# DeltaNet inverse at levels 4 and 5: packed diagonal 64x64 blocks, and all four turns behind all four y products

## The reference

```python
CHUNK = 64
kb = k * beta[..., None]
lmat = jnp.where(strict, jnp.einsum('nbhid,nbhjd->nbhij', kb, k) * decay, 0.0)
amat = lmat + jnp.eye(CHUNK, dtype=F32)
rhs = jnp.concatenate([v * beta[..., None], kb * jnp.exp(gcum)[..., None]], axis=-1)
sol = lax.linalg.triangular_solve(amat, rhs, left_side=True, lower=True, unit_diagonal=True)
u, w = sol[..., :dv], sol[..., dv:]
def step(s, xs):
    v_new = u_i - jnp.einsum('bhcd,bhde->bhce', w_i, s)
    o = jnp.einsum('bhcd,bhde->bhce', qg_i, s) + jnp.einsum('bhij,bhje->bhie', attn_i, v_new)
    s = s * gl_i[..., None, None] + jnp.einsum('bhcd,bhce->bhde', kd_i, v_new)
    return s, o
```

## Time and profile before

| | us |
|---|---|
| median of 3 runs | 3374.56 (3374.05 to 3378.11) |
| profiled execution, own time | 3373.96 |
| its span, first to last instruction | 3372.1 |
| TensorE busy | 3216.7 (95%) |
| VectorE busy | 2492.9 (74%) |
| ScalarE busy | 1346.5 (40%) |
| GpSimd busy | 277.0 (8%) |
| first DeltaNet layer, first y product to last oi product | 565.6 to 679.1 |
| second DeltaNet layer, the same | 2905.1 to 3018.5 |

### The profile page before, as it was taken

How to read it: one execution, slowest core, us unless ns; L and a number is a source line. 1 busy time by engine, 2 the same in 40 slices (tenths; PEclk the granted TensorE clock), 3 DMA queues, 4 the chain that set the end, 5 groups by cost and what they waited for, 6 DMA issues and landing times.

```text
span 3372.1 us, 50038 instructions
## 1 busy us (share of the span) xinstructions
PE 3216.7 (95%) x17956; PEld 2998.1 (89%) x17956; DVE 2492.9 (74%) x4217; ACT 1346.5 (40%) x2398; POOL 277.0 (8%) x373
## 2 busy tenths in 40 slices
PE   7999898989999999899999999999999999899997
PEld 7899898979999998868999998899999898888997
DVE  7888976667887885567887887788788886666444
ACT  2333556243334334354334333433433365533332
POOL 1000004510000000000000000000000000640000
PEclk9999999999999999999999999999999999999999
DMA  7555310044544553214553554355445431013331
GB/s 292 218 198 211 142 71 1 26 163 187 205 181 187 218 205 136 102 41 185 204 219 142 207 218 160 147 198 216 181 187 208 160 129 52 26 48 134 120 122 75
DMA packets 66032, 515.99 MB, mean 153 GB/s; under 512 B 8144, under 2 KB 16336, under 8 KB 18048
## 3 DMA queue, kind: packets, MB, share of 16 engines
q1 hardware_dynamic: 60512, 493.12, 38.0%
q0 software_dynamic: 5408, 21.37, 1.7%
HBM read 509.65 MB, written 4.82 MB: 153 GB/s over the span
## 4 chain that ended last, share of the span: by engine, by line
PE 87%; DVE 7%; ACT 2%; issue 1%; DMA 1%; SPq 0%; POOL 0%; DVEq 0%; POOLq 0%; ACTq 0%
PE bank L1774 76%; PE bank L1964 5%; DVE xhat L1359 1%; DMA mod_raw<-mod_w 1%; DVE x L1363 1%; PE bank L1970 1%; PE bank L2072 1%; DVE split_lo L1209 1%; PE bank L1915 1%; DVE mod_junk L434 1%; PE bank L1822 0%; DVE xS_lo L1302 0%; PE bank L1826 0%; DVE blocks L1478 0%; PE bank L1823 0%
## 5 line engine op out<-in xcount | busy, mean ns | idle before, releaser
L1774 PE MATMUL bank<-xS_hi,split_hi 128*128 128x386 f32 (+2 forms) x3280 | 1120.2, 342 | 13.5 <-DVE gate_n L1325 10.2
L1774 PE MATMUL bank<-xS_hi,split_lo 128*128 128x386 f32 (+2 forms) x3280 | 1111.0, 339 | 0.0
L1774 PE MATMUL bank<-xS_lo,split_hi 128*128 128x386 f32 (+2 forms) x3280 | 1109.8, 338 | 0.0
L1209 DVE TENSOR_TENSOR split_lo<-raw,split_hi 128x1024 fp32r<-128x1024 f32 x644 | 778.7, 1217 | 263.2 <-ACT split_hi L835 263.2
L835 ACT ACTIVATE split_hi<-raw 128x1024 fp32r<-128x1024 f32 x644 | 652.6, 1051 | 490.0 <-DMA raw<-ffn_w 347.8
L434 DVE SCALAR_TENSOR_TENSOR mod_junk<-mod_raw,cond 128x1024 f32<-128x1024 f32 x536 | 655.7, 1223 | 62.7 <-DVE mod_junk L434 36.1
L1774 PEld LDWEIGHTS bank<-xS_hi,split_hi 128*128 128x128 f32 (+1 forms) x3280 | 617.4, 188 | 28.8 <-DVE split_lo L1209 10.6
L1774 PEld LDWEIGHTS bank<-xS_lo,split_hi 128*128 128x128 f32 (+1 forms) x3280 | 618.5, 189 | 9.9 <-issue 0.4
L1774 PEld LDWEIGHTS bank<-xS_hi,split_lo 128*128 128x128 f32 (+1 forms) x3280 | 618.6, 189 | 1.0
L1774 PE MATMUL bank<-split_hi,hid_hi 128*128 128x512 f32 x1056 | 413.2, 391 | 1.6 <-DVE hid_lo L1337 1.6
L1774 PE MATMUL bank<-split_lo,hid_hi 128*128 128x512 f32 x1056 | 412.9, 391 | 0.0
(11 more groups left out here) (277 smaller groups left out, 3209.2 us busy)
## 6 DMA issues: line engine op xcount, KB each, us to landing
raw<-ffn_w SPq DMA_DIRECT2D x176, 1536.0 KB, 7.6
mod_raw<-mod_w SPq DMA_DIRECT2D x134, 1024.0 KB, 4.8
raw<-a_in_w SPq DMA_DIRECT2D x20, 1536.0 KB, 6.4
gate_bc<-gate_dram POOLq DMA_DIRECT2D x12, 1024.0 KB, 5.3
raw<-b_in_w SPq DMA_DIRECT2D x8, 1536.0 KB, 6.3
raw<-a_out_w SPq DMA_DIRECT2D x4, 1536.0 KB, 8.1
mod_first<-mod_w SPq DMA_DIRECT2D x5, 1024.0 KB, 21.9
mod_first<-mod_rows SPq DMA_DIRECT2D x5, 1024.0 KB, 23.9
```

The costliest lines, as they stand in the source:

```text
L1209: dve.tensor_tensor(split_lo[:, unit.slot, q, 0:w], raw[:, unit.slot, q, 0:w], f32(split_hi[:, unit.slot, q, 0:w]), ALU.subtract).then_inc ...
L1774: ins = pe.matmul(out, lhsT, rhs, start=start and i == 0, stop=stop and i == 2)
```

## The change

At levels 4 and 5 only the two 64x64 blocks on the diagonal of each 128x128 matrix hold anything. The changed kernel stores and computes these alone. A packed quad is 128 x 256: rows 0 to 63 hold the four first blocks, rows 64 to 127 the four second ones. Two packed quads share one 128 x 512 tile. `diagonal` issues, per head, one 64x64 product for the first halves (rows 0 to 63 of the array, output partitions 0 to 63) and one for the second halves (rows 64 to 127, output partitions 64 to 127), in the same PSUM bank and the same columns of it. At level 6 the full matrix is put together in `W_S`: its diagonal blocks come from level 5's subtraction (j < 2) or from the turn (j >= 2), one off-diagonal block is minus the z product, and the other one is set to zero once per layer by POOL. The other changes follow: masks are 64 wide, `expanded` writes half as much, and the POOL tiles of the next wave all wait for z6 (before, C waited for y6). Per level TensorE does the four y products first, then the four turns.

```diff
+    W_S = wk[0:4]
+    packed = lambda slots: [wk[s][:].rearrange("p (u h) c -> p u (h c)", u=2)[:, u].rearrange("p (h c) -> p h c", h=GROUP)
+                            for s in slots for u in range(2)]
+    P_C, P_B = packed((4, 5)), packed((6, 7))
     W_Y = wk[8:12]
+    P_Y = packed((8, 9, 10, 11))[::2]
...
     # GpSimd
             for j in range(4):
-                expanded(pool, W_B[0][j], bc, j, 0, block_mask).then_inc(w_pool[j], 1)
+                expanded(pool, P_B[j], bc, j, 0, block_mask).then_inc(w_pool[j], 1)
+            pool.wait_ge(w_pool[3], event("pool", 3, a, 0, "be"))
+            for j in range(4):
+                rows_of, cols_of = (SECOND, FIRST) if j < 2 else (FIRST, SECOND)
+                steps.settle(pool.memset(W_S[j][rows_of, :, cols_of], 0.0))
...
             def spread_next(w):
-                for j in range(4):
-                    mm(j, w, "y6")
-                    expanded(pool, W_C[w + 1][j], cc, j, w + 1, block_mask).then_inc(w_pool[j], 1)
-                for j in range(4):
-                    mm(j, w, "z6")
-                    expanded(pool, W_B[w + 1][j], bc, j, w + 1, block_mask).then_inc(w_pool[j], 1)
+                for compact, tiles in ((cc, P_C), (bc, P_B)):
+                    for j in range(4):
+                        mm(j, w, "z6")
+                        expanded(pool, tiles[j], compact, j, w + 1, block_mask).then_inc(w_pool[j], 1)
...
     # ScalarE
-                for lev in LEVELS[:-1]:
-                    for j in range(4):
-                        mm(j, f"t{lev}")
-                        act.activation(W_B[w][j].rearrange("p h c -> p (h c)"), ps[4 + j][:], ACT.Copy).then_inc(w_act[j], 1)
+                for j in range(4):
+                    mm(j, "t4")
+                    act.activation(P_B[j], turned_half(j, slice(0, P)), ACT.Copy).then_inc(w_act[j], 1)
+                for j in range(4):
+                    mm(j, "t5")
+                    if j < 2:
+                        act.activation(P_B[j][FIRST], turned_half(j, FIRST), ACT.Copy).then_inc(w_act[j], 1)
+                    else:
+                        act.activation(W_S[j][FIRST, :, FIRST], turned_half(j, FIRST), ACT.Copy)
+                        act.activation(W_S[j][SECOND, :, SECOND], turned_half(j, SECOND), ACT.Copy).then_inc(w_act[j], 1)
...
     # VectorE
-                            ins = dve.tensor_copy(W_Y[j][FIRST, :, SECOND], bank(j)[FIRST, :, SECOND])
+                            ins = dve.tensor_copy(P_Y[j][FIRST], half_bank(j, FIRST))
                         else:
-                            ins = dve.tensor_tensor(W_Y[j][:], bank(j), per_head(level_mask[lev - LEVELS[0]]), ALU.mult)
+                            ins = dve.tensor_tensor(P_Y[j], half_bank(j), per_head(level_mask[lev - LEVELS[0]]), ALU.mult)
...
                         if lev == LEVELS[-1]:
+                            rows_of, cols_of = (FIRST, SECOND) if j < 2 else (SECOND, FIRST)
+                            ins = dve.tensor_scalar(W_S[j][rows_of, :, cols_of], half_bank(4 + j, rows_of), -1.0, None, ALU.mult)
+                        elif lev == LEVELS[1] and j < 2:
+                            dve.tensor_tensor(W_S[j][SECOND, :, SECOND], P_C[j][SECOND], half_bank(4 + j, SECOND), ALU.subtract)
+                            ins = dve.tensor_tensor(W_S[j][FIRST, :, FIRST], P_C[j][FIRST], half_bank(4 + j, FIRST), ALU.subtract)
+                        else:
+                            ins = dve.tensor_tensor(P_C[j], P_C[j], half_bank(4 + j), ALU.subtract)
...
     # TensorE
+            def diagonal(bank, lhsT, rhs, halves_of=(FIRST, SECOND)):
+                for h in range(GROUP):
+                    for half in halves_of:
+                        ins = pe.matmul(ps[bank][half, h * HALF:(h + 1) * HALF], lhsT(half, h), rhs(half, h), start=True, stop=True)
                 return ins
...
-                        four(j, lambda h: amap[:, i + h], lambda h: W_C[w][j][:, h]).then_inc(w_mm[j], 1)
+                        diagonal(j, lambda half, h: amap[half, i + h, half], lambda half, h: P_C[j][half, h]).then_inc(w_mm[j], 1)
...
-                        ins = four(4 + j, lambda h: W_B[w][j][:, h], lambda h: W_Y[j][:, h])
+                        ins = diagonal(4 + j, lambda half, h: P_B[j][half, h], lambda half, h: P_Y[j][half, h])
...
                 for lev in LEVELS:
                     for j in range(4):
                         y_product(j, lev)
-                        if lev > LEVELS[0]:
-                            turn(j)
+                    for j in range(4 if lev > LEVELS[0] else 0):
+                        turn(j, lev)
```

More of the change, by code:

```diff
@@ L47 @@
 LEVELS = (4, 5, 6)
-FIRST, SECOND = slice(0, P // 2), slice(P // 2, P)
+HALF = P // 2
+FIRST, SECOND = slice(0, HALF), slice(HALF, P)
 WAVES = 3
@@ L269, in build @@
     mod_first = [place(f"mod_first{i}", [P, MOD_TILES, D], at=at) for i, at in enumerate(mod_at)]
[L271 to L274, removed]
+    dn_const = place("dn_const", [P, 6 * HALF], at=region_m + 8 * KB)
+    level_mask = [dn_const[:, HALF * i:HALF * i + HALF] for i in range(2)]
+    block_mask = dn_const[:, 2 * HALF:3 * HALF]
+    neg_ident, above, below = (dn_const[:, HALF * i:HALF * i + HALF].bitcast(BF16) for i in (3, 4, 5))
     cc = place("cc", [P, 2, BLK, 32], at=region_m)
@@ L469, in of_wave @@
         return maps[:, i:i + GROUP]
-    W_C = [[wk[j][:] for j in range(4)]] + [[of_wave(amap, w, j) for j in range(4)] for w in range(2)]
-    W_B = [[wk[4 + j][:] for j in range(4)], [wk[4 + j][:] for j in (0, 1)] + [wk[j][:] for j in (2, 3)],
-           [wk[4 + j][:] for j in (0, 1)] + [of_wave(amap, 0, j) for j in (2, 3)]]
+    W_V = [[of_wave(amap, w, j) for j in range(4)] for w in range(2)]
     first_sq = att[:, 0:HEADS]
@@ L1551, in delta_net @@
                     dve.wait_ge(w_act[j], event("act", j, a, w, "vn"))
-                    dve.tensor_tensor(solved(w, j), bank(j if w else 4 + j), small(SM_EKD, CHUNK_OF[w][d], d, quad),
+                    dve.tensor_tensor(W_V[w][j], bank(j if w else 4 + j), small(SM_EKD, CHUNK_OF[w][d], d, quad),
                                       ALU.mult).then_inc(w_dve[j], 1)
@@ L2025, in delta_net @@
             pe.wait_ge(small_ready, a + 1)
-            pe.matmul(ps[7][:, 0:P], ident[:], block_mask, start=True, stop=True).then_inc(mask_copied, 1)
+            pe.matmul(ps[7][:, 0:HALF], ident[:], block_mask, start=True, stop=True).then_inc(mask_copied, 1)
             for w in range(WAVES):
@@ L2061, in z_product, with turn @@
                     if lev < LEVELS[-1]:
-                        ins = four(4 + j, lambda h: W_B[w][j][:, h], lambda h: W_Y[j][:, h])
+                        ins = diagonal(4 + j, lambda half, h: P_B[j][half, h], lambda half, h: P_Y[j][half, h])
                     elif j < 2:
-                        ins = quarter(4 + j, FIRST, SECOND, lambda h: W_B[w][j][FIRST, h, FIRST], lambda h: W_Y[j][FIRST, h, SECOND])
+                        ins = quarter(4 + j, FIRST, lambda h: P_B[j][FIRST, h], lambda h: P_Y[j][FIRST, h])
                     else:
-                        ins = quarter(4 + j, SECOND, FIRST, lambda h: W_Y[j][FIRST, h, SECOND], lambda h: W_B[w][j][FIRST, h, FIRST])
+                        ins = quarter(4 + j, SECOND, lambda h: P_Y[j][FIRST, h], lambda h: W_S[j][FIRST, h, FIRST])
                     ins.then_inc(w_mm[j], 1)
-                def turn(j):
-                    for h in range(GROUP):
-                        ins = pe.transpose(ps[4 + j][:, h * P:(h + 1) * P], W_C[w][j][:, h], ident[:])
+                def turn(j, lev):
+                    eye = lambda half, h: ident[half, half]
+                    if lev == LEVELS[-1] and j < 2:
+                        ins = diagonal(4 + j, lambda half, h: W_S[j][half, h, half], eye, (FIRST,))
+                    else:
+                        ins = diagonal(4 + j, lambda half, h: P_C[j][half, h], eye)
                     ins.then_inc(w_mm[j], 1)
@@ L2103, in delta_net @@
                     dv(j, "vs")
-                    four(4 + j, lambda h: dn_k[:, CHUNK_OF[w][d], GROUP * quad + h], lambda h: solved(w, j)[:, h]).then_inc(w_mm[j], 1)
+                    four(4 + j, lambda h: dn_k[:, CHUNK_OF[w][d], GROUP * quad + h], lambda h: W_V[w][j][:, h]).then_inc(w_mm[j], 1)
                 pe.wait_ge(att_done, 2 * N_MAP * a + (2 * N_MAP if w else 4))
```

35 lines of the change are left out of this document (19 added, 16 removed).

## The result

The changed kernel took 3348.06 us (median of 4 runs, 3345.68 to 3348.9) against 3374.68 us (4 runs). The ratio is 0.9918, 95% interval 0.9901 to 0.9935. A repetition beside the experiments gave 3344.01 us (5 runs, 3342.42 to 3351.13), ratio 0.9909 (0.9896 to 0.9923). So the change saves 27 to 31 us, 0.8 to 0.9%. The forecast was 39 us, 3335. Direction and range were right, the gain was two thirds to four fifths of the forecast.

The account below looks back on a forecast made before the run. TensorE was taken to bound the waves. Per layer 5.2 + 7.5 + 7.3 = 20.0 us for the three waves, less 0.4; twice 19.6 is 39 us off 3373.96, giving 3335 us, range 3326 to 3380.

Parts of the forecast that it names:

- TensorE is the bound of the waves: In waves 1 and 2 TensorE is busy throughout, so a microsecond taken from it is one of the kernel.
- The halves run side by side: Packed products at levels 4 and 5: both 64x64 halves overlap in full, 0.457 us per product; chance 0.60.
- The first rival: Packed products: the halves take turns in one bank, 0.915 us each, kernel slower at 3385 us; chance 0.15.
- the second rival: Packed products: the halves overlap only partly, 0.68 us each, a wave 19.5, kernel 3355 us; chance 0.18.
- The third rival: Waves: 64x64 work does not hold TensorE at 2.4 GHz; at 1.2 GHz throughout, 3412 us; chance 0.07.
- The turns take two passes: Packed 64x64 turns need two fp32 passes, so get no cheaper: 0.457 us per quad, 0.44 before.
- A wave without holes takes 15.5 us: Waves 1 and 2: 14.63 us of products and turns, 0.4 for starts and shape changes, 0.5 waiting for VectorE.
- The change puts y6 together and makes all of level 6 64x64: Level 6: about 0.15 us saved at eight places; y6 and t5 take 1.83 us each.
- The smaller engines: VectorE 0.41 us per 128x256 operation, ScalarE copies about 0.4, GpSimd tiles 4 x 0.80 and memsets 4 x 0.35.
- I take 0.4 off for a wave 0 that stands idle 3 us and may start vn at a lower clock: Wave 0: TensorE waits 3.1 us for GpSimd, vn starts 5.2 us earlier; 0.4 deducted per layer for a lower clock.
- (23.05 - 15.5): Wave 1 falls from 23.05 to 15.5 us, saving 7.5 us per layer.
- What follows each wave is only moved: From ks to oi, then norm and output weights behind each wave: shifted in time, with no gain or cost.

Follow-up runs that it names:

- x3: Changed kernel with each packed product issued as four first halves, then four second halves, instead of alternating: 3349.56 us, one run.
- x4: Changed kernel with each turn right behind its own y product, still packed: 3345.75 us.
- x1: Changed kernel with GpSimd's last 4 of 12 attention-map operations moved behind wave 0's right-hand sides and wave 1's tiles: 3334.27 us.
- x2: Changed kernel with the reload of the state (two 512 KB transfers) held back until y5 of wave 1 is done: 3341.59 us.
- x9: x7 with each state reload bringing one head of eight, so it doesn't compute what the others do: 3327.74 us.
- x8: Kernel before, unpacked, with the edits of x1 and x2 (maps behind, reload held back to y5): 3375.95 us, ratio 0.9992 to 1.0010.
- x5: Kernel before, nothing packed, with only the new order (four y products, then four turns) at levels 5 and 6: 3373.80 us.
- x6: Changed kernel with the edits of x1 and x2 together (maps behind, reload held back to y5): 3334.82 us.
- x10: x7 with the state's reload held back further, to z5 of wave 1 instead of y5: 3331.13 us.
- x7: Changed kernel with the edits of x1, x2 and x4 together (maps behind, reload at y5, turns behind their y): 3331.16 us.

## Why the prediction was right or wrong

**TensorE is the bound of the waves: right**, and it stayed so in wave 2. It was not so in wave 0, and that was forecast.

**The halves run side by side: right.** 0.465 us per product against 0.457 forecast. The first rival (halves take turns, 0.915) and the second (0.68) are out by the 64 rows in 1.86 us. The rule that I weighed (the Trainium skill, TensorEngine Tiling (Array Packing), Restrictions and Gotchas, Gotcha 1) says that different row tiles cannot access the same PSUM bank simultaneously. This trace does not agree with it for halves that write different partitions of the bank. x3 goes halfway to the second rival with 0.575, by the order of issue alone. So the order two-and-two was a part of the gain, of which I had only said that it "is inside what these rows show".

**The third rival, a lower clock under 64x64 work: wrong as a rival.** The granted clock of waves 1 and 2 is 1.00.

**The turns take two passes: right**, 64 rows for four turns.

**A wave without holes takes 15.5 us: right** for wave 2 (15.6; the gain is 7.2 of 7.3). The 0.5 at its head is there as well: the second y product starts 0.95 us after the first (598.25 to 599.20), 0.48 more than a product, behind VectorE's copy. For y6 behind z5's double operations I had 0.1, it is 0.27.

**"The change puts y6 together and makes all of level 6 64x64": half right.** The changes of shape went, but I took the four y6 as 1.83 us of unpaired rows and the turns as 1.83 behind them, and never priced the old order in the packed kernel. x4 shows that there it is 1.2 us per wave cheaper, since a y6 row and a turn's row can run side by side.

**The smaller engines: right.** VectorE 0.416 to 0.424 (forecast 0.41), ScalarE 0.384 (0.4), GpSimd's tiles 3.32 for four (3.2), memsets 1.39 (1.4), first right-hand side ready at about 585.6 (585.0; 0.4 of the difference is that GpSimd started at 564.98, not 564.59).

**Wave 0: mechanism right, term mis-sized.** I forecast 3.1 us of idle TensorE; it was 3.47. The step that failed is "I take 0.4 off for a wave 0 that stands idle 3 us and may start vn at a lower clock". The clock did fall, in both layers of both profiles of this kernel, and vn alone took 1.3 us (first layer) and 2.1 us (second) more than in the earlier trace rows. Of the 5.2 us forecast per layer 3.05 and 2.2 were left. x1 shows that one cause stands behind both: without the wait the clock stayed at 1.00.

**Wave 1: the step that failed is "(23.05 - 15.5)", a wave without holes, taken over to a wave in which a transfer runs.** It took 17.3 us (598.25 to 615.58) instead of 15.5: 5.7 gained of 7.5. 1.49 of the missing 1.8 is the hole. It was 1.10 to 1.55 in the other layer and in the repetition. I had said under the second rival that loads and matmuls "must be handed out at twice the rate", and had looked only at whether the array takes them. I never asked whether the instructions arrive. x2 and x9 show that the hole hangs on the state's reload, and the times of the instruction packets say that it is the instructions that come late; x8 shows that the old wave never noticed.

The terms of the first layer add up: 3.05 + 5.7 + 7.2 = 16.0 of 19.6, and the stretch gives 15.9. For both layers it is 31.3 of 39.2.

**"What follows each wave is only moved": not shown wrong.** The first profile has 6.1 us more outside the stretches than before, the repetition 1.7. In kernels that alter nothing there, the rest goes from 3143.0 to 3151.4 us, and x5, nearly the kernel before, has 3150.0. What differs in the rows read here are stretches with more time at the lower clock, as over the norm and output weights behind wave 2 (0.91 in the changed kernel's profile, 0.93 in the repetition's, 0.95 before, 95 us each). They fall differently from profile to profile, and runs of one kernel lie 1 to 16 us apart. Whether the changed kernel has a constant cost of 1 or 2 us there stays open.

The time forecast for the change is what x1 takes, 3334.27 us, but by another sum: with GpSimd out of the way wave 0 gives more than the 5.2 us that I had left it, the hole in wave 1 takes some back, and its stretches give 114.2 + 114.1 - 94.1 - 93.4 = 40.8 us.

## What to carry to other kernels

Before forecasting what a faster stage brings, look up who stands just behind TensorE now: GpSimd had 3.7 us of slack and 14.8 us of work with no hurry in front of work that the next product needs. Putting four operations behind it was worth 10 to 14 us of kernel time (9.5 in the stretches), a third to a half of what the whole change had brought. And count instructions, not only their durations: if the same work is handed out in rows half as long, two of them side by side, the fetch of instructions comes due four times as often as the profile of before shows, and a large transfer that was free of cost can hold it up.

Block-diagonal fp32 products are worth packing as pairs of 64x64 products in one PSUM bank, first half and second half in turn. Where a 64x64 product has no partner, put it next to work on the other half of the array. An order that is good for the kernel before is to be priced again in the packed one.

## What the runs showed of the hardware

- Two 64x64 fp32 products on different rows of the array and different output partitions overlap in full in one PSUM bank: 16 rows in 0.465 us, against 0.057 for each. With the four products of one half ahead of the four of the other it is 0.575 (x3). Unpaired products and turns on different rows of the array that write the same partitions of different banks overlap too: y6 and t5 took 2.94 us in turn and 3.95 one behind the other (x4).
- A change between 64x64 and 128x128 shape costs some 0.14 us: six of them fewer brought 0.86 us per wave in x5.
- TensorE stood 1.1 to 2.0 us for its next 16 KB of instructions when two 512 KB transfers had been under way, at about 34 matmul rows and as many weight loads per us; in x3, at about 28, it stood 0.2 us or not at all. An eighth of the bytes takes the hole away (x9), and so does holding the transfer back far enough (x2, x6, x10, but not x7).
- Behind 3.3 to 3.5 us of idle TensorE the next 5 to 6 us had a granted clock of 0.60 to 0.68; without the idle time it was 1.00 in the same place (x1). Idle time of 1.2 to 1.3 us there was enough for 0.69 (x3, x9, x10), while behind holes of 1.1 to 2.0 us in level 5 of wave 1 the clock stayed at 1.00 (changed kernel, x1, x4). Behind 1.9 us in level 6 it was 0.50 (x7). What makes the difference stays open.
- The granted clock falls in other places from one profile to the next, and the rest of this kernel's span moves by up to 8 us, in part with it. Differences under that are read from a stretch of the trace, not from the median.
